# Strassen's seven products in the first product of a SwiGLU feed-forward, for ten of eleven column groups

## The reference

```
u = rms_norm(x, pre_norm)                       # 512 x 1024
gate, up = split(u @ w_in)                      # w_in 1024 x 5632, so 2 x 2816 columns
y = (silu(gate) * up) @ w_out                   # w_out 2816 x 1024
x = x + 0.5 * rms_norm(y, post_norm)
```

## Time and profile before

| | us |
|---|---|
| median of 3 runs | 2223.99 (2223.95 to 2224.84) |
| profiled execution, its span | 2220.7 |
| between span and median | 3.3 |

### The profile page before, as it was taken

One profiled execution on the slowest core, in us unless ns is written; L12 is line 12 of the kernel. 1 busy time (PEld: TensorE's weight loads), 2 busy tenths in 40 slices (PEclk: granted clock), 3 DMA queues, 4 the chain that ended last, 5 costly groups with the idle time before them and its releaser, 6 DMA issues. The chain is left out here.

```text
span 2220.7 us, 28711 instructions
## 1 busy us (share of the span) xinstructions
PE 2195.2 (99%) x11172; PEld 1834.3 (83%) x11172; DVE 1039.6 (47%) x1475; ACT 838.0 (38%) x1482; POOL 74.6 (3%) x104
## 2 busy tenths in 40 slices
PE   7999999999999999999999999999999999999998
PEld 6888888888888888888888888887888888888887
DVE  4545424695536544342353433256945455444323
ACT  4323214655533523231252322156554425333211
POOL 0000001010000100000000000010100001000000
PEclk9999999999999999999999999999999999999999
DMA  5332222332123222322233222323321243222222
GB/s 212 95 104 95 95 95 86 124 84 77 58 85 136 101 96 94 104 94 95 86 105 104 94 95 95 101 82 121 88 71 59 86 146 100 97 95 94 98 101 76
DMA packets 72566, 217.91 MB, mean 98 GB/s; under 512 B 19217, under 2 KB 19729, under 8 KB 71697
## 3 DMA queue, kind: packets, MB, share of 16 engines
q1 hardware_dynamic: 70448, 203.92, 28.0%
q0 software_dynamic: 2016, 12.58, 1.6%
HBM read 208.87 MB, written 7.60 MB: 97 GB/s over the span
## 5 line engine op out<-in xcount | busy, mean ns | idle before, releaser
L1369 DVE TENSOR_TENSOR wlo<-raw,whi 128x1024 fp32r<-128x1024 f32 (+1 forms) x375 | 457.6, 1221 | 869.3 <-ACT whi L954 858.1
L537 PE MATMUL ps<-uhi,whi 128*128 128x512 f32 (+1 forms) x2144 | 808.2, 377 | 3.0 <-DVE wlo L1369 1.6
L539 PE MATMUL ps<-uhi,wlo 128*128 128x512 f32 (+1 forms) x2144 | 800.5, 373 | 0.0
L538 PE MATMUL ps<-ulo,whi 128*128 128x512 f32 (+1 forms) x2144 | 800.5, 373 | 0.0
L954 ACT ACTIVATE whi<-raw 128x1024 fp32r<-128x1024 f32 (+1 forms) x372 | 390.7, 1051 | 901.9 <-PE ps L539 520.2
L537 PEld LDWEIGHTS ps<-uhi,whi 128*128 128x128 f32 x2144 | 403.7, 188 | 76.9 <-issue 3.8
L539 PEld LDWEIGHTS ps<-uhi,wlo 128*128 128x128 f32 x2144 | 403.6, 188 | 71.8
L538 PEld LDWEIGHTS ps<-ulo,whi 128*128 128x128 f32 x2144 | 403.8, 188 | 69.8
L612 PE MATMUL ps<-whi,hhi 128*128 128x512 f32 x704 | 274.4, 390 | 0.0
L614 PE MATMUL ps<-whi,hlo 128*128 128x512 f32 x704 | 273.9, 389 | 0.0
L613 PE MATMUL ps<-wlo,hhi 128*128 128x512 f32 x704 | 273.9, 389 | 0.0
(11 more groups left out here) (236 smaller groups left out, 1666.2 us busy)
## 6 DMA issues: line engine op xcount, KB each, us to landing
raw<-in_wstream_dram SPq DMA_DIRECT2D x367, 512.0 KB, 3.3
x_home<-x POOLq DMA_DIRECT2D x4, 1024.0 KB, 4.3
x<-x_home POOLq DMA_DIRECT2D x2, 2048.0 KB, 8.5
gain<-in_gp_dram POOLq DMA_DIRECT2D x6, 512.0 KB, 4.7
raw<-in_wstream_dram SPq DMA_DIRECT2D x10, 256.0 KB, 3.9
xT<-in_xt_dram SPq DMA_DIRECT2D x8, 256.0 KB, 6.0
x<-in_x_dram SPq DMA_DIRECT2D x4, 512.0 KB, 8.3
out_dram<-x SPq DMA_DIRECT2D x8, 256.0 KB, 2.0
```

The costliest lines, as they stand in the source:

```text
L537: pe.matmul(o, lh, bhi, start=first, stop=False)
L538: pe.matmul(o, lh, blo, start=False, stop=False)
L539: return pe.matmul(o, ll, bhi, start=False, stop=last)
L1369: dve.tensor_tensor(wlo[:, s, 0:cols], raw[:, s % RAWS, 0:cols], whi[:, s, 0:cols].bitcast(f32), ALU.subtract) \
```

## The change

For groups 1 to 10 the product of a group is seen as a 2 x 2 block product: weights in four blocks W_11 (k tiles 0 to 3, gate columns), W_12 (k 0 to 3, up), W_22 (k 4 to 7, up), W_21 (k 4 to 7, gate), each 128 x (4 x 256), and tokens in four blocks (k half by 256 tokens). Instead of eight block products there are seven, in Winograd's variant of Strassen's scheme; a block product is 2 column tiles x 4 k tiles x 3 matmuls with 256 tokens. The new parts:

- **Weights.** The blocks come whole in float32 from an array `swstream` of their own, four DMAs of 512 KB per group. DVE makes four sums of them (`sum_3`, `sum_11`, `sum_22`, `sum_4`). The seven operands (`Q_A`, `Q_D`, `Q_B`, `Q_A2`, `Q_C`, `Q_D2`, `Q_C2`, in this order) are rounded by ACT (`unit_round`), and DVE writes the rest in place (`unit_rest`). There are 8 slots for lo and 5 for hi, some of which lie in the old rings, and one in the part of `uhi` that is no longer read.
- **Tokens.** Once per feed-forward POOL adds hi and lo back together (`whole_u`, four operations of 128x1024), DVE makes four combinations (`combine`), which are split in hi and lo like weights (`combined_round`, `combined_rest`).
- **Results.** The sums of products are made in PSUM: a bank is copied into another as the start of the next accumulation (`keep_a` with the sign turned, `keep_b`), or kept in SBUF and subtracted (`keep_d`, `y22`, `y21`). Silu and up work on halves of 256 tokens (`first_tanh`, `first_gate`, `first_h`, `second_tanh`, `second_h`), in (0,0) with four more DVE operations for `rb`. Their result, `hf`, stays in float32; `h_round` and `h_rest` split it, for k = 0 to 2 at the end of the last group and for the others one per chunk in the second product.
- Before group 1 PE makes two dummy matmuls that mark two banks as written. `first_out` is group 0's silu; in ACT's and DVE's queues it stands within group 1. The loops over groups are gone: all queues are straight. `head_group`, `first_group`, the second product, the boundary and the mixer keep their matmuls.

The core of the diff (of SP the waits for g > 1):

```diff
-A_CHUNKS = (FT // 2) * (KT // 2)
+A_CHUNKS = KT // 2
...
+UNITS = 7
+FAST = FINAL * UNITS
+LO_SLOTS, HI_SLOTS = 8, 5
...
+        LO_AT, HI_AT = (136, 140, 152, 156, 148, 180, 168, 172), (56, 160, 176, 164)
...
+                for g in range(FIRST, GROUPS):
...
+                    load_part(L, f, g, W_11, whole(f, g, Q_A))
...
+                        sp.wait_ge(*of_group(sum11, L, f, g - 1))
+                        sp.wait_ge(*of_group(sum3, L, f, g - 1))
+                    load_part(L, f, g, W_12, r12[:, :, :])
...
+                    load_part(L, f, g, W_22, r22[g % 2])
...
+                    load_part(L, f, g, W_21, whole(f, g, Q_A2))
...
+            def tokens_of(u, k):
+
+                if u in (Q_D, Q_B, Q_C, Q_C2):
+                    i = {Q_D: S_3, Q_B: S_2, Q_C: S_1, Q_C2: S_4}[u]
+                    return chi[i][:, k, :], clo[i][:, k, :]
+                row = {Q_A: 0, Q_A2: 4, Q_D2: 4}[u] + k
+                cols = slice(2 * P, 4 * P) if u == Q_D2 else slice(0, 2 * P)
+                return uhi[:, row, cols], ulo[:, row, cols]
+
+            def product(f, g, u):
+
+                hi, lo = operand(f, g, u)
+                b = role(g, {Q_A: 0, Q_D: 3, Q_B: 1, Q_A2: 0, Q_C: 2, Q_D2: 3, Q_C2: 2}[u])
+                for i in range(2):
+                    o = bank(b, 2 * P * i, 2 * P)
+                    for k in range(4):
+                        lh, ll = hi[:, k, i * P:(i + 1) * P], lo[:, k, i * P:(i + 1) * P]
+                        bhi, blo = tokens_of(u, k)
+                        pe.matmul(o, lh, bhi, start=u in (Q_A, Q_D) and i == 0 and k == 0, stop=False, skip_group_check=True)
+                        pe.matmul(o, lh, blo, start=False, stop=False, skip_group_check=True)
+                        last = pe.matmul(o, ll, bhi, start=False, stop=True, skip_group_check=True)
+                return last
+
+            def fast_group(L, f, g):
+                def combined(i):
+                    if g == 1:
+                        pe.wait_ge(c_lo.h, c_lo.at(L, 4 * f + i + 1))
+
+                if g == 1:
+                    for i in (1, 2):
+                        pe.matmul(bank(role(g, i)), uhi[:, 4, 0:P], uhi[:, 4, :], start=True, stop=True, skip_group_check=True)
+                pe.wait_ge(*of_unit(unit_lo, L, f, unit_no(g, Q_A)))
+                if g == 2:
+                    pe.wait_ge(tile_read.h, tile_read.at(L, TILE_A[f] + 4))
+                elif g > 2:
+                    pe.wait_ge(*of_group(gate1, L, f, g - 2))
+                product(f, g, Q_A).then_inc(unit_done.h, 1)
+                pe.wait_ge(*of_unit(unit_lo, L, f, unit_no(g, Q_D)))
+                combined(S_3)
+                if g > 2:
+                    pe.wait_ge(*of_group(y21_done, L, f, g - 2))
+                product(f, g, Q_D).then_inc(unit_done.h, 1)
+                pe.wait_ge(*of_unit(unit_lo, L, f, unit_no(g, Q_B)))
+                combined(S_2)
+                pe.wait_ge(*of_move(SEED_B, L, f, g))
+                product(f, g, Q_B).then_inc(unit_done.h, 1)
+                pe.wait_ge(*of_unit(unit_lo, L, f, unit_no(g, Q_A2)))
+                product(f, g, Q_A2).then_inc(unit_done.h, 1)
+                pe.wait_ge(*of_unit(unit_lo, L, f, unit_no(g, Q_C)))
+                combined(S_1)
+                pe.wait_ge(*of_move(SEED_C, L, f, g))
+                product(f, g, Q_C).then_inc(unit_done.h, 1)
+                pe.wait_ge(*of_unit(unit_lo, L, f, unit_no(g, Q_D2)))
+                pe.wait_ge(*of_move(KEPT_D, L, f, g))
+                product(f, g, Q_D2).then_inc(unit_done.h, 1)
+                pe.wait_ge(*of_unit(unit_lo, L, f, unit_no(g, Q_C2)))
+                combined(S_4)
+                pe.wait_ge(*of_group(y22_done, L, f, g))
+                product(f, g, Q_C2).then_inc(unit_done.h, 1)
...
-                group_in(1, 1)
-                group_in(2, 0)
-                with pe.Fori(3, FT // 2 - 1, 2) as it:
-                    group_in(it, 1)
-                    group_in(it + 1, 0)
+                for g in range(FIRST, GROUPS):
+                    fast_group(L, f, g)
...
+            def keep_a(L, f, g):
+
+                act.wait_ge(*of_unit(unit_done, L, f, unit_no(g, Q_A)))
+                if g == 2:
+                    free_of_first(L, f)
+                act.activation(bank(role(g, 1)), bank(role(g, 0)), ACT.Copy, scale=-1.0).then_inc(moved.h, 1)
+
+            def keep_d(L, f, g):
+
+                act.wait_ge(*of_unit(unit_done, L, f, unit_no(g, Q_D)))
+                if g == 1:
+                    free_of_first(L, f)
+                else:
+                    act.wait_ge(*of_group(h2_done, L, f, g - 1))
+                act.activation(tmp[:, 1, :], bank(role(g, 3)), ACT.Copy).then_inc(moved.h, 1)
+
+            def keep_b(L, f, g):
+
+                act.wait_ge(*of_unit(unit_done, L, f, unit_no(g, Q_B)))
+                if g > 2:
+                    act.wait_ge(*of_group(h1_done, L, f, g - 2))
+                act.activation(bank(role(g, 2)), bank(role(g, 1)), ACT.Copy).then_inc(moved.h, 1)
+                act.activation(tmp[:, 0, :], bank(role(g, 1)), ACT.Copy).then_inc(moved.h, 1)
+
...
+                unit_round(L, f, 1, Q_A)
+                combined_round(L, f, S_3)
+                combined_round(L, f, S_2)
+                if (L, f) == (0, 0):
+                    act.wait_ge(rb_made.h, 1)
+                    act.activation(rb[:, :], bank(4), ACT.Copy).then_inc(rb_out.h, 1)
+                unit_round(L, f, 1, Q_D)
+                for g in range(FIRST, GROUPS):
+                    if g > 1:
+                        second_tanh(L, f, g - 1)
+                    unit_round(L, f, g, Q_B)
+                    unit_round(L, f, g, Q_A2)
+                    if g == 1:
+                        combined_round(L, f, S_4)
+                        combined_round(L, f, S_1)
+                        first_out(L, f)
+                    keep_a(L, f, g)
+                    unit_round(L, f, g, Q_C)
+                    keep_d(L, f, g)
+                    unit_round(L, f, g, Q_D2)
+                    unit_round(L, f, g, Q_C2)
+                    keep_b(L, f, g)
+                    if g == FINAL:
+                        h_round(L, f, 0)
+                        h_round(L, f, 1)
+                    first_tanh(L, f, g)
+                    if g < FINAL:
+                        unit_round(L, f, g + 1, Q_A)
+                        unit_round(L, f, g + 1, Q_D)
...
+            def sum_3(L, f, g):
+
+                dve.wait_ge(*of_part(W_12, L, f, g))
+                dve.wait_ge(*of_part(W_22, L, f, g))
+                if g > 1:
+                    dve.wait_ge(*of_unit(unit_done, L, f, unit_no(g, Q_D) - LO_SLOTS))
+                dve.tensor_tensor(whole(f, g, Q_D), r12[:, :, :], r22[g % 2], ALU.add).then_inc(sum3.h, 1)
...
+            def unit_rest(L, f, g, u):
+
+                hi, lo = operand(f, g, u)
+                dve.wait_ge(*of_unit(unit_hi, L, f, unit_no(g, u)))
+                if u == Q_C2:
+                    if g == 1:
+                        dve.wait_ge(gemm_done.h, gemm_done.at(L, UNIT_A[f] + 4))
                     else:
...
+                        dve.wait_ge(*of_unit(unit_done, L, f, unit_no(g, u) - LO_SLOTS))
+                dve.tensor_tensor(lo, whole(f, g, u), hi.bitcast(f32), ALU.subtract).then_inc(unit_lo.h, 1)
...
+            def combine(L, f, i):
+
+                dve.wait_ge(u_whole.h, u_whole.at(L, 4 * f + (2, 3, 4, 3)[i]))
+                if i == S_3:
+                    ins = dve.tensor_tensor(cf[S_3][:, :, :], part_of_u(0), part_of_u(2), ALU.subtract)
+                elif i == S_2:
+                    dve.wait_ge(c_sum.h, c_sum.at(L, 4 * f + S_3 + 1))
+                    ins = dve.tensor_tensor(cf[S_2][:, :, :], cf[S_3][:, :, :], part_of_u(3), ALU.add)
...
+            def y22(L, f, g):
+
+                dve.wait_ge(*of_unit(unit_done, L, f, unit_no(g, Q_C)))
+                dve.wait_ge(*of_move(KEPT_D, L, f, g))
+                dve.tensor_tensor(tmp[:, 1, :], bank(role(g, 2)), tmp[:, 1, :], ALU.subtract).then_inc(y22_done.h, 1)
+
+            def y21(L, f, g):
+
+                dve.wait_ge(*of_unit(unit_done, L, f, unit_no(g, Q_D2)))
+                dve.wait_ge(*of_move(KEPT_R, L, f, g))
+                dve.tensor_tensor(tmp[:, 0, :], bank(role(g, 3)), tmp[:, 0, :], ALU.subtract).then_inc(y21_done.h, 1)
+                if (L, f) == (0, 0):
+                    dve.wait_ge(*of_group(y21_done, L, f, g))
+                    dve.tensor_tensor(wide(tmp[:, 0, :]), wide(tmp[:, 0, :]), rb_half(1), ALU.mult).then_inc(gs2_done.h, 1)
...
+                sum_11(L, f, 1)
+                unit_rest(L, f, 1, Q_A)
+                sum_3(L, f, 1)
+                combine(L, f, S_3)
+                sum_22(L, f, 1)
+                combine(L, f, S_2)
+                combined_rest(L, f, S_3)
+                combine(L, f, S_4)
+                combined_rest(L, f, S_2)
+                combine(L, f, S_1)
```

(120 more changed lines are left out.)

350 lines of the change are left out of this document (234 added, 116 removed).

## The result

| | before | after |
|---|---|---|
| median, us | 2223.97 (4 runs) | 2210.52 (4 runs, 2208.61 to 2212.64) |
| span of the profiled execution, us | 2220.7 | 2210.8 |
| mean granted clock of it | 0.999 | 0.988 |

The ratio is 0.9937, 95% interval 0.9923 to 0.9951: 0.6% faster. The forecast was 0.19% faster (2219.7), so the sign and the range (2202 to 2239) held, but the gain is three times the one forecast: 9 us of it were not foreseen. In five more runs on another chip the ratio was 0.9941 (0.9928 to 0.9955).

What follows compares the result with a forecast made beforehand. TensorE (PE), busy 99% of the span, was taken as the bound. Terms -64.1 + 36.6 + 21.7 + 1.5 = -4.3 us took the span from 2220.7 to 2216.4, the median to 2219.7; range 2202 to 2239.

Steps and rivals of the forecast that it cites:

- The saving: Ten groups per feed-forward: 201.6 us in place of 217.6, 16.0 less each, 64.1 us in all four.
- The openings: Before group 1 of three later feed-forwards: PE waits 9.2 us for D, 2.9 for C; 12.2 each, 36.6 in all.
- the POOL piece: One whole_u operation of 128x1024 in the openings: 2.54 us, its time adding to DVE's.
- the loss at low clock: After PE's wait for D: 1.5 us lost in (0,0); in three openings the next wait (2.9) swallows it.
- (0,0): First feed-forward: waits of 11.4 us for D, 5.3 for B, 0.3 for C, plus 4.7 in running groups; 21.7 us.
- The mixers: Mixer stretches between feed-forwards: no term in the sum, so 520.4 and 519.9 us as before.
- granted clock below 1 in these places only: Sign: clock falls only where PE waits before D of group 1 (9 to 10 us) and before C (some 3).
- Span and median: Whole kernel: median of the runs 3.3 us above the profiled span, so 2219.7 from 2216.4.
- 1a: Openings: a POOL piece costs 1.27 us; -21 us, 2203; chance 0.10.
- 1b: Openings: POOL and DVE run side by side, D ready at 778.6; -38 us, 2186; chance 0.07.
- Rival 2: (0,0): VectorE paces it with a round of 22.4 us, openings 0.9 longer; +15 us, 2239; chance 0.17.
- Rival 3: Fast groups: 256-column matmuls don't hold 0.120 us; 122 ns gives 2232, 129.5 ns gives 2283; chance 0.09.

Runs made afterwards that it cites:

- The experiment with rb: Changed kernel with ACT copying rb ahead of the roundings of S_3 and S_2, in (0,0) only: 2211.17 us, ratio 0.9944.
- the DRAM experiment: Changed kernel with an unused 1.25 MB DRAM tensor in front of the one through which the mixer's solve gathers its blocks: 2210.07 us, ratio 0.9940.
- D first: Changed kernel with DVE doing D's rest three operations earlier in every opening, ACT's roundings in the same order: 2213.76 us, ratio 0.9962.
- the extra operation: Changed kernel with one more DVE addition of 128x1024, result not used, in eight groups of every feed-forward: 2218.79 us, ratio 0.9975.
- the first try: Changed kernel with openings rearranged: new DVE order, POOL making two token sums and DVE the others, group 1 buffer, earlier rb copy: 2196.28 us, ratio 0.9872.
- three pieces on DVE: Changed kernel with the last three of each feed-forward's four POOL additions done by DVE: 2199.01 us, ratio 0.9885.
- the last rearranged kernel: The first try with S_2's rounding and group 1's y22 earlier, and group 2's rests of A and D before group 1's first_gate: 2179.44 us, ratio 0.9803.

## Why the prediction was right, and where it was off

- **The saving.** Right: 168 matmuls of 256 columns in 20.16 us, in 27 of 27 groups after the first of the later feed-forwards. The 2.5 ns that the Trainium skill (TensorE: Matmul & The Clock Gate, "Wait — 56ns, not 53.3ns?") adds to N / 2.4 GHz stays short of these rows, which show 13 ns. (By that rule the saving would be 95 us; the prediction has 94.)
- **The openings.** Mechanism right: moving POOL's pieces to DVE gave what the row of work said, and taking them away gave it less 1.5 us of clock. Mis-sized was the POOL piece: 2.2 us of blocking, not 2.54, and a wait of 7.3 for D (with the dummies ahead of it 7.8, forecast 9.2). From D to C 11.6 us passed, 11.5 had been forecast. The extra in each later feed-forward was 10.8 us and not 12.2: 4.2 us of the gain. That the loss at low clock lies in front of the wait for keep_b and vanishes in it was right: D to C is 11.62 us in the second feed-forward, where the low clock covers 3.9 us of it and C waits 1.0, and 11.62 in the third, where it covers 6.2 and C hardly waits.
- **(0,0).** The sum was too high by 6.3 us, and one wait was missed. The forecast had PE wait 11.4 for D; it waited 7.1 for rb ahead of A, because the copy of rb waits in ACT's queue behind two roundings that DVE releases. The experiment with rb shows that this wait only stands in for that for D. D's rest was done at 47.5, not 50.7. The prediction left the split of 27.98 in DVE's row, but that is a chunk of group 1, which the changed kernel doesn't split; the last split of the head group came at 23.2, and DVE did sum_11 before POOL's first piece at 27.2. So two of the twelve operations fell out of the row, and the four pieces cost 0.34 less each. B waited 3.4 (forecast 5.3), the low clock took 3.6 in group 1 and some 0.5 of the dummies' 1.0 (forecast 1.5), and the running groups lost 1.8 (forecast 4.7: the first three kept PE's pace, the rest ran at 20.47, not 20.68). 7.1 + 1.0 + 3.4 + 3.6 + 1.8 = 16.9 in place of 23.2.
- **The mixers.** Missed altogether: +5.1 us in this execution, 4.9 with the stretch between that has none. The prediction had nothing there but equal code. What is shown: in all ten profiles with the change the issue behind the solve's gather takes SP 3.1 to 3.7 us in the first mixer (1.95 before), a chunk lands later and PE waits 1.0 to 1.9 us in place of 0.6; in six of the ten the clock falls in this mixer. The stretch takes 521.0 and 521.3 us in two profiles where it doesn't fall (the DRAM experiment and "D first") and 523.8 and 524.0 in those of the changed kernel, against 520.4 before: the clock is the larger part. In the second mixer this issue takes 2.0 to 2.1 us as before, yet PE waits 0.85 to 1.0 in place of 0.6, and in five of the ten the clock falls there. The prediction's sign "granted clock below 1 in these places only" thus didn't hold. Why the issue takes longer stays open; an unused tensor in front of the gathered one didn't change it.
- **Span and median.** The prediction put 3.3 us between them. Every run shows 1.8 (2212.64 and 2210.8); the other 1.5 was that the profiled execution of before was a quick one, while that of after was 2.1 slower than its median. From -4.3: -4.2 - 6.3 + 4.9 = -9.9 in the span, and - 1.5 - 2.1 = -13.5 in the median.
- **Rivals.** 1a and 1b are refuted by the 3.42 us rows. Rival 2 didn't come; the extra operation showed its place. Rival 3 (at 122 ns its sum gives 2233, not 2232) is refuted by the 20.16 us groups.

The chances leaned too much on the upper side: the terms for (0,0) were each taken at the unfavourable end (0.05 for every hand-over, 2.54 for a piece), and with the split that isn't there they gave 6 us. The openings and (0,0) came out 10.5 us under the forecast; that the mixers, which it had at nothing, took back 4.9 was luck for the number.

## What to carry to other kernels

When an edit puts new work in front of a stage, add up all of it up to the last queue that the stage needs (here C's seed), not up to the first wait: shortening the longest wait moved it and gained nothing, while shortening the row of work gained nearly all that was taken out. An idle engine isn't free help if its operations block the engine that sets the time: 1.14 us on DVE was cheaper here than 2.2 us of POOL, while in the boundary, beside operations that read PSUM, POOL was free. And after rearranging, look at the trace again: the first try got half of the 31 us that the new order was worth, and mending what its trace showed got the other half (ratios 0.9941, 0.9872, 0.9803).

## What was unexpected of the hardware

- **Taking turns.** Three POOL operations of 2.4 us alone and three DVE operations of 1.2 interleave one by one (9.99 us for the three on POOL, 3.42 for each on DVE). Of a piece's 2.39 us 2.2 are added to DVE's time, so next to nothing overlaps.
- **The clock after short waits.** Behind the waits of 7.1 us the clock is at 1.2 GHz for 3.9, 6.2 and 6.0 us of D and B in the three openings of one profile. In the first mixer it fell at PE waits of 1.41 and 1.51 us (two profiles of the changed kernel), of 1.37 twice and of 1.90 ("rb first", "three pieces on DVE", the extra operation), and didn't fall at waits of 1.72 and 1.73 (the DRAM experiment, "D first" and the last rearranged kernel). The wait doesn't decide this alone, and what else does was not found. Where it fell in the changed kernel's profiles, the stretch took 2.5 to 3 us more than in the two variants above where it didn't, which fits the spread of 4 to 5 us among its runs, though only the profiled ones show where the clock fell. The last rearranged kernel, without long waits, spreads by 2.7.
